# The sum of the second row blocks and the residual of down by accumulating transfers, and a new order of first casts and sums in a Strassen-Winograd feed-forward network

## What is computed

```python
h = x + jnp.concatenate([a, c], axis=-1) @ w_out
n2 = rms_norm(h, norm_ffn)
h = h + (jax.nn.silu(n2 @ w_gate) * (n2 @ w_up)) @ w_down
# D_MODEL 2048, D_FF 5632, 544 tokens
y = rms_norm(h, norm_final)
```

## Time and profile before

| | us |
|---|---|
| time, median of 3 runs | 2389.84 (2389.76 to 2390.09) |
| the profiled execution | 2386.59 |
| its span, first to last instruction | 2384.9 |
| TensorE busy | 2285.8 (96%) |
| VectorE busy | 1830.2 (77%) |
| ScalarE busy | 991.9 (42%) |
| POOL busy | 496.6 (21%) |
| share of the 16 DMA engines, SP's queue and POOL's | 40.7% and 3.8% |

### The profile page before, as it was taken

How to read it: one execution, slowest core, us unless ns; L and a number is a source line. 1 busy time by engine, 2 the same in 40 slices (tenths; PEclk the granted TensorE clock), 3 DMA queues, 4 the chain that set the end, 5 groups by cost and what they waited for, 6 DMA issues and landing times.

```text
span 2384.9 us, 48272 instructions
## 1 busy us (share of the span) xinstructions
PE 2285.8 (96%) x17572; PEld 2192.5 (92%) x17572; DVE 1830.2 (77%) x2648; ACT 991.9 (42%) x1409; POOL 496.6 (21%) x528
## 2 busy tenths in 40 slices
PE   7999999999989997999999999999999789999898
PEld 6977999998759997999999999999999789989898
DVE  5688999997624558877777777778777788888897
ACT  6154344333532224444444444444444343443444
POOL 2324899650550102010100101010010000000000
PEclk9999999999999998999999999999999899999999
DMA  7414223323695452443444434444344653444543
GB/s 260 119 35 124 73 79 85 88 71 95 199 310 166 126 148 80 125 125 104 132 124 125 130 106 122 124 131 127 111 116 126 205 186 99 139 146 135 150 107 102
DMA packets 455375, 307.42 MB, mean 129 GB/s; under 512 B 23195, under 2 KB 436371, under 8 KB 454576
## 3 DMA queue, kind: packets, MB, share of 16 engines
q1 hardware_dynamic: 443472, 276.73, 40.7%
q0 software_dynamic: 11792, 29.23, 3.8%
HBM read 269.56 MB, written 37.18 MB: 129 GB/s over the span
## 4 chain that ended last, share of the span: by engine, by line
PE 55%; DVE 3%; issue 2%; ACT 1%; DMA 0%; POOL 0%; DVEq 0%; POOLq 0%; SPq 0%; ACTq 0%
PE ps L2452 54%; ACT opH L1160 1%; DVE wr L1843 1%; DVE opH L1869 1%; DVE h L1989 0%; DVE opX L1795 0%; DVE wl L1852 0%; PE ps L2501 0%; DVE wp L1819 0%; DMA h<-xT_dram 0%; ACT opX L1127 0%; POOL td L830 0%; DVE ws L1843 0%; DVE wr L1812 0%; DVE t L1900 0%
## 5 line engine op out<-in xcount | busy, mean ns | idle before, releaser
L2452 PE MATMUL ps<-opX,wp 128*128 128x272 f32 x7392 | 937.0, 290 | 12.1 <-ACT t L1170 9.5
L2452 PEld LDWEIGHTS ps<-opX,wp 128*128 128x128 f32 x7392 | 936.0, 189 | 12.8 <-ACT t L1170 9.9
L2452 PE MATMUL ps<-opH,wh 128*128 128x272 f32 x2464 | 468.9, 290 | 36.8 <-DVE h L1989 33.3
L1819 DVE TENSOR_TENSOR wp<-wr,wp 128x1024 fp32r<-128x1024 f32 x264 | 320.1, 1226 | 188.2 <-ACT wp L1143 185.9
L2452 PEld LDWEIGHTS ps<-opH,wh 128*128 128x128 f32 x2464 | 389.8, 190 | 40.6 <-DVE h L1989 36.6
L2074 PE MATMUL ps<-xs,whi 128*128 128x272 f32 (+1 forms) x2368 | 396.2, 289 | 6.4 <-DVE xs L1318 2.3
L2452 PE MATMUL ps<-opH,wl 128*128 128x272 f32 x1232 | 356.7, 290 | 0.0
L1143 ACT CAST wp<-wr 128x1024 fp32r<-128x1024 f32 x264 | 273.6, 1053 | 181.6 <-DVE wr L1812 140.0
L2074 PEld LDWEIGHTS ps<-xs,whi 128*128 128x128 f32 (+1 forms) x2368 | 334.7, 187 | 9.3 <-DVE xs L1318 2.8
L1154 ACT CAST wh<-wr 128x768 fp32r<-128x768 f32 (+1 forms) x192 | 149.8, 781 | 251.8 <-PE ps L2452 178.2
L2074 PE MATMUL ps<-xs,wlo 128*128 128x272 f32 (+1 forms) x1184 | 244.7, 288 | 0.0
(11 more groups left out here) (335 smaller groups left out, 2674.8 us busy)
## 6 DMA issues: line engine op xcount, KB each, us to landing
wr<-in_w_gate SPq DMA_DIRECT2D x88, 512.0 KB, 4.6
wr<-in_w_up SPq DMA_DIRECT2D x88, 512.0 KB, 7.1
raw<-in_w_in SPq DMA_DIRECT2D x72, 512.0 KB, 3.9
wr<-in_w_down SPq DMA_DIRECT2D x96, 384.0 KB, 5.4
rawH<-hid_dram SPq DMA_DIRECT2D x21, 816.0 KB, 6.7
raw<-in_w_out SPq DMA_DIRECT2D x32, 512.0 KB, 5.3
hid_dram<-hid SPq DMA_DIRECT2D x88, 136.0 KB, 1.8
hid_dram<-td SPq DMA_DIRECT2D x66, 136.0 KB, 1.8
```

The costliest lines, as they stand in the source:

```text
L1819: ve.tensor_tensor(w[:, 1, :, :], src[:, :, :], w[:, 0, :, :].bitcast(F32), ALU.subtract).then_inc(s_wlo, 1)
L2452: ins = te.matmul(prod_bank(par, i), w[:, t, :], op[:, x, t, :], start=(i in (0, 1, 3) and t == 0 and w is whi_ and x == 0), stop=(t == kk ...
```

## The change

Three parts.

At the start of gate and up, ScalarE squares tile 14 first, casts pieces 4 and 5 before the weights of unit 2, and takes unit 0's result earlier. VectorE sums and splits in a matching order, and does B21 - B11 in one operation of 2176 columns; POOL's two operations for it go.

In the first group of down, h isn't loaded first. ScalarE copies the results of units 0, 1, 2 and 6 into h (`placed`), VectorE adds units 3, 4 and 5, and POOL then adds the residual of each two tiles from `xT_dram` by an accumulating transfer (`residual_added`), one per pair. SP's three transfers go. The first additions of the second group wait for them.

In all of down, POOL fills ws2: a transfer of block 2, a wait, an accumulating transfer of block 3 (`second_row_sum`). It waits until VectorE has used the ws2 of the pair before. VectorE's sum for it goes. SP loads the same four blocks as before.

```diff
+        def adds(p):
+            return 3 * min(p, NP2) + 7 * max(p - NP2, 0)
...
-            sp.wait_ge(s_prod, fed(NP1 - 1, 6))
-            sp.dma_start(h[:, 0:2, :], xT_dram[:, 0:2, :]).then_inc(s_xr[0], 16)
-            sp.dma_start(h[:, 2:8, :], xT_dram[:, 2:8, :]).then_inc(s_xr[1], 16)
...
-            sp.dma_start(h[:, 8:16, :], xT_dram[:, 8:16, :]).then_inc(s_hl, 16)
...
-            operand_sums(B21, B21, B11, ALU.subtract, 0, 7)
-            pool.wait_ge(s_opl, 8)
-            operand_sums(B21, B21, B11, ALU.subtract, 7, 8)
...
+            def second_row_sum(p):
+                ws = ws2[:, 0:KG[p // NP2], :]
+                if p == 0:
+                    pool.wait_ge(s_wlo, fed(NP1 - 2, 6))
+                else:
+                    pool.wait_ge(s_wlo, fed(NP1 + p - 1, 1))
+                    pool.wait_ge(s_wsum, sums2(p - 1) + 2)
+                pool.dma_start(ws, down_block(p, 2)).then_inc(s_ws, 16)
+                pool.wait_ge(s_ws, AT_SW + 32 * p + 16)
+                pool.dma_start(ws, down_block(p, 3), accum_op=ALU.add).then_inc(s_ws, 16)
+            def residual_added(i):
+                if i:
+                    pool.wait_ge(s_hres, AT_SW + 16 * i)
+                pool.wait_ge(s_hcp, 4 * i + 4)
+                pool.wait_ge(s_hacc, adds(i + 1))
+                pool.dma_start(h[:, 2 * i:2 * i + 2, :], xT_dram[:, 2 * i:2 * i + 2, :], accum_op=ALU.add
+                               ).then_inc(s_hres, 16)
+            second_row_sum(0)
             hid_sums(NB2 - 1)
+            second_row_sum(1)
+            for s in range(2):
+                pool.wait_ge(s_xw[s], AT_XW + 16 * 8)
+            for p in range(2, 4 * NP2):
+                second_row_sum(p)
+                if p < NP2 + 2:
+                    residual_added(p - 2)
...
+            square_of(14, 0)
             weight_high1(0, 0, 0, 1)
-            square_of(14, 0)
             weight_high1(0, 1, 0, 1)
-            weight_high1(0, 2, 0, 1)
...
             piece_high(6)
+            taken(t1[:, 0:HALF], 0, 0, 0)
+            weight_high1(0, 2, 0, 1)
             piece_high(7)
+            weight_high1(0, 3, 0, 1)
...
+            def placed(p, k):
+                e, n, t = p % 2, NP1 + p, 2 * p
+                unit_, tile_, half = ((0, t, slice(0, HALF)), (1, t + 1, slice(HALF, NT)), (2, t, slice(HALF, NT)),
+                                      (6, t + 1, slice(0, HALF)))[k]
...
+                act.wait_ge(s_prod, fed(n, unit_))
+                nc.scalar.copy(h[:, tile_, half], prod_bank(e, unit_)).then_inc(s_hcp, 1)
...
+                    if c == 0 and v in (0, 1, 2, 6):
+                        placed(p, min(v, 3))
...
-                dst, x, z, op = ((ws2, raw4[2], raw4[3], ALU.add), (raw4[2], raw4[0], raw4[2], ALU.subtract),
-                                 (raw4[0], ws2, raw4[0], ALU.subtract), (raw4[1], raw4[1], raw4[0], ALU.subtract))[k]
+                dst, x, z = ((raw4[2], raw4[0], raw4[2]), (raw4[0], ws2, raw4[0]), (raw4[1], raw4[1], raw4[0]))[k]
...
-            weight_sum1(0, 2, 0)
             piece_low(4)
             piece_low(5)
             dve.wait_ge(s_mm, 2 * M_FFN)
             residual(15, 1, 16 * 8)
-            for x in range(6, 8):
-                piece_low(x)
+            weight_sum1(0, 2, 0)
+            piece_low(6)
             weight_low1(0, 2, 0)
+            piece_low(7)
+            weight_low1(0, 3, 0)
+            piece_low(8)
+            weight_low1(0, 4, 0)
+            weight_sum1(0, 3, 0)
+            dve.wait_ge(s_xd, 8)
+            dve.wait_ge(s_opl, 9)
+            ve.tensor_tensor(B21, B21, B11, ALU.subtract).then_inc(s_xd, 1)
+            piece_low(9)
...
-                    else:
+                    elif c or v in (3, 4, 5):
                         gathered(p, v)
...
+                if c == 0:
+                    dve.wait_ge(s_hcp, 4 * p + after)
+                elif after:
+                    dve.wait_ge(s_hacc, adds(p) + after)
+                elif c == 1:
+                    dve.wait_ge(s_hres, AT_SW + 16 * (i + 1))
```

More of the change, by code:

```diff
@@ L69 @@
 NPIECE = 11
-AT_OPD = AT_HL = 32 * 6
+AT_OPD = AT_SW = 32 * 6
 AT_WR = 32 * 8
@@ L320, in build @@
         s_ho0, s_ho = s_iks[2:4]
-        s_hl = s_pg[9]
         s_opd = s_pg[2:9]
-        s_hacc = sem("s_hacc")
+        s_hacc, s_hcp = sem("s_hacc"), sem("s_hcp")
+        s_hres, s_ws = s_pgp[2:4]
         s_gf, s_yt, s_ya, s_yd = (sem("s_" + x) for x in ("gf", "yt", "ya", "yd"))
@@ L491, in op_slot, with sums2, down_block @@
             return (7 * c + j) % 9
+        def adds(p):
+            return 3 * min(p, NP2) + 7 * max(p - NP2, 0)
+        def sums2(p):
+            return 4 * NP1 + 3 * p
+        def down_block(p, b):
+            c, i = divmod(p, NP2)
+            return w_down[:, b % 2, KG0[c]:KG0[c] + KG[c], 256 * i + P * (b // 2):256 * i + P * (b // 2) + P]
         def fed(n, i):
@@ L1148, in weight_high2 @@
                 act.wait_ge(s_prod, fed(n, i) - (3 if v > 2 else 4))
-                if SUM[i]:
-                    act.wait_ge(s_wsum, 4 * n + SUM[i])
+                if i == 1:
+                    act.wait_ge(s_ws, AT_SW + 32 * p + 32)
+                elif SUM2[i]:
+                    act.wait_ge(s_wsum, sums2(p) + SUM2[i])
                 else:
@@ L1205, in pair1 @@
                 after = extra or (lambda k: None)
-                taken(t1[:, 0:HALF], par, 0, n)
-                weight_high1(par, 3, n, fill)
+                if extra is not first_extra:
+                    taken(t1[:, 0:HALF], par, 0, n)
+                    weight_high1(par, 3, n, fill)
                 after(0)
@@ L1253, in final_square @@
             def final_square(j):
-                act.wait_ge(s_hacc, 7 * (3 * NP2 + j // 2) + (6, 7)[j % 2])
+                act.wait_ge(s_hacc, adds(3 * NP2 + j // 2) + (6, 7)[j % 2])
                 act.wait_ge(s_sqs, KT + 2 + max(j - 1, 0))
                 nc.scalar.activation(sqf[:, j % 2, :], h[:, j, :], ACT.Square).then_inc(s_sqh, 1)
+            def placed(p, k):
+                e, n, t = p % 2, NP1 + p, 2 * p
+                unit_, tile_, half = ((0, t, slice(0, HALF)), (1, t + 1, slice(HALF, NT)), (2, t, slice(HALF, NT)),
+                                      (6, t + 1, slice(0, HALF)))[k]
+                if k == 0 and p == 5:
+                    act.wait_ge(s_ho0, AT_HO + 16 * NB2)
+                    act.wait_ge(s_ho, AT_HO + 96 * NB2)
+                act.wait_ge(s_prod, fed(n, unit_))
+                nc.scalar.copy(h[:, tile_, half], prod_bank(e, unit_)).then_inc(s_hcp, 1)
             for p in range(4 * NP2):
@@ L1904, in pair1 @@
                 after = extra or (lambda k: None)
-                weight_low1(par, 3, n)
-                weight_sum1(par, 3, n)
-                after(0)
-                weight_low1(par, 4, n)
-                after(1)
+                if extra is not first_extra:
+                    weight_low1(par, 3, n)
+                    weight_sum1(par, 3, n)
+                    after(0)
+                    weight_low1(par, 4, n)
+                    after(1)
                 weight_low1(par, 5, n)
@@ L2488, in _ @@
                 else:
-                    pe.wait_ge(s_hacc, 7 * (p - 1))
+                    pe.wait_ge(s_hacc, adds(p - 1))
+                    if p < NP2 + 2:
+                        pe.wait_ge(s_hcp, 4 * (p - 1))
                 for i in range(7):
-                    if i in (2, 4, 5, 6):
-                        pe.wait_ge(s_hacc, 7 * p + (1, 3, 3, 5)[(2, 4, 5, 6).index(i)])
+                    if c == 0:
+                        if i in (2, 4):
+                            pe.wait_ge(s_hcp, 4 * p + i - 1)
+                        if i == 6:
+                            pe.wait_ge(s_hacc, adds(p) + 2)
+                    elif i in (2, 4, 5, 6):
+                        pe.wait_ge(s_hacc, adds(p) + (1, 3, 3, 5)[(2, 4, 5, 6).index(i)])
                     if p % NP2 == 0:
```

58 lines of the change are left out of this document (20 added, 38 removed).

## The result

The changed kernel takes **2409.8 us** (median of 4 runs, 2403.2 to 2411.8) against 2389.8 before: ratio 1.0076, 95% interval 1.0063 to 1.0089. It is slower by 20 us where 12.6 us of gain were forecast. Its profiled execution, 2403.17 us with a span of 2401.3, is the fastest of the four, so it shows 16.6 us of the loss against the profiled execution of before (2386.59). The page of the changed kernel: share of the span by engine, transfers by queue, issues with KB each and us to landing.

What follows compares the result with a forecast made beforehand. TensorE was taken as full in mid-stage, so only some 48 us of its gaps could be had. 4.5 + 5.1 - 3 + 4.8 + 4.2 - 3 = 12.6 us gained, from 2389.84 to 2377 us; range 2364 to 2410.

Steps and rivals of the forecast that it cites:

- the first change of group: Down, first cluster of gaps: ScalarE's copies and one sum less on VectorE gain 4.8 us, 1 us charged for late landings.
- the other two: Down, second and third change of group: VectorE's sum goes, 2.1 us each, 4.2 gained, 1 us charged per change.
- the third term: Down, the new loop through ws: a loss of 3 us in the forecast's sum.
- Part 1: Start of gate and up: VectorE's one-piece difference and reordered casts bring low parts earlier; gain 4.5 us, bounds 2.5 and 6.9.
- Part 2: Entry of down: the 12.03 us gap shrinks, then ws of pair 1 is late; gain 5.1 us of 8.7, bounds 0 and 10.
- Part 3: Down: two-transfer ws loop just fits the first group's pairs; 0.5 us lost per pair over six, 3 us, bounds 0 and 13.
- Part 4: Down, three changes of group: less VectorE work gains 4.8 and 4.2 us, 1 us charged per change, 3 us.
- What was called free: Down: dropped SP residual transfers, POOL's new waits, the second group's residual wait and TensorE's changed waits were said to cost nothing.
- The slower one: Down: accumulates take 7 and 9.5 us, ws paces every pair, 27 us lost, about 2409 us; chance 0.26.

Runs made afterwards that it cites:

- e10: Kernel before with only the new start of gate and up (difference of B21 on VectorE, ScalarE's new order of casts): 2386.6 us, ratio 0.9993.
- e1: Changed kernel without the eight accumulating residual transfers in the first group of down: 2396.3 us, ratio 1.0029.
- e8: Changed kernel with the two ws transfers of pair 1 moved ahead of POOL's last sums of hid: 2407.7 us, ratio 1.0085.
- e2: Changed kernel with all sums into ws2 back on VectorE, the adding residual kept: 2379.2 us, ratio 0.9956.
- e7: Changed kernel with all ws sums back on VectorE and the adding residual moved from the first group to the second: 2375.5 us, ratio 0.9940.
- e5: Changed kernel with the second transfer of ws plain, overwriting instead of adding: 2395.1 us, ratio 1.0024.
- e4: Changed kernel with the residual's accumulating transfers moved from the first group to the second: 2403.8 us, ratio 1.0067.
- e3: Changed kernel with VectorE summing ws in the first group only, POOL's transfers in the later groups: 2385.4 us, ratio 0.9980.

## Why the prediction was wrong, point by point

The forecast's sum against what the profiled executions show, us gained: the start 4.5 and 5.0; the entry 5.1 and -0.5; the loop -3 and -17.4; the first change of group 4.8 - 1 and -3.9; the other two 4.2 - 2 and, with all later lengths, -0.5. With 1 us from the stage ahead that is -16.3. The failed step is the third term.

**Part 1, the start: right at its place.** 4.0 us measured with part 1 alone (e10), 5.0 in the changed kernel, 4.5 said; that they reach the end isn't shown. VectorE's 4.48 us piece beside POOL is gone; the changed kernel's timeline of VectorE at that place:

```profile
916.10 0.43 DVE L1842 TENSOR_TENSOR opX<-hg,opX 128x272 fp32r<-128x272 f32 x1
916.45 1.22 DVE L1866 TENSOR_TENSOR wp<-wr,wp 128x1024 fp32r<-128x1024 f32 x1
918.13 2.42 DVE L1842 TENSOR_TENSOR opX<-hg,opX 128x2176 fp32r<-128x2176 f32 x1 [0.46 <-ACT opX L1157]
```

**Part 2, the entry: the mechanism right, the gain not.** Without ws on POOL's queue the first two lengths fall from 36.5 to 28.2 us, 8.3 of the 8.7 said. With it they are 36.9: nothing gained, where 5.1 were said. I let ws of pair 1 land 3.4 + 4.8 us after POOL got free. I had placed the wait right (a gap of 4.51 us through a cast of ws), but the adding transfer was issued in the same microsecond as SP's loads of pair 2 and took 7.7 us. In e1, with no residual at all, it took 7.5 at this place, so it is stretched beside SP's loads without the residual. The changed kernel, transfers issued from 1868.0 to 1868.2 us:

```profile
wr<-in_w_down SPq DMA_DIRECT2D x2, 256.0 KB, 3.2
ws<-in_w_down POOLq DMA_DIRECT2D x1, 256.0 KB, 7.7
```

I had read SP's next loads at 1880.5, the time of before, and didn't move them forward with the entry that the change itself moves. e8 shows the place: there length 1 is 5.7 us shorter. A second length of 11.4 instead of 10.5 took another 0.9.

**Part 3, the loop through ws: this step failed.** The prices of the transfers were right, undisturbed 4.4 to 5.0 us for 256 KB (4.8 said) and 5.5 to 6.0 for 384 KB (6.2 said). So was the claim that the middle of the later groups hides the loop: 22 lengths sum to 364.9 against 364.4. (One price was right by luck: the 0.4 us for POOL's issue don't follow from their row. By the same working 128 KB from SP land after 2.3 us and POOL's after 2.4, which is 0.1 us more.) What failed is the first group: 3 us charged, with a bound of 13; lengths 3 to 6 alone lost 17.4 us. Two terms were wrong, the second far more.
- The loop: 10.9 us, not 10.4. From landing to the next issue it takes 2.7 us in e1 (1886.81 to 1889.50 us), not 2.2, and POOL needs 0.3 us between the two transfers, which I had left out. That alone puts it above a pair's 10.50. By itself it is what the 0.5 us per pair were charged for: lengths 3 to 5 of e1 lose 1.3 us together.
- The engines' time, which I never summed. I compared landings taken from undisturbed rows and read "39% busy" as room. SP's loads of one pair, in the kernel before, over 10.5 us (1889 to 1899.5):

```profile
q1 hardware_dynamic: 2112, 1.05, 34.2%
```

That is 3.6 us of the engines. The plain ws takes 1.0 and the adding one 2.2. The adding residual, in e2 over 6.4 us (1882.2 to 1888.6), its 272 packets, partly beside SP's:

```profile
q0 software_dynamic: 272, 0.56, 57.4%
```

3.7 us, and about the same in e7 (56.5% of 6.5 us from 2020.3) with hardly any other traffic. The sum is 10.5 us in a pair of 10.5. The changed kernel agrees: 75% of 42 us for 262 matmuls is 10.1 us of the engines for a pair's 84 matmuls.

With a pair's time on the engines all taken, transfers meet in every pair, and landings stretch. The changed kernel, transfers issued from 1907.6 to 1908.0 us:

```profile
wr<-in_w_down SPq DMA_DIRECT2D x2, 256.0 KB, 3.3
ws<-in_w_down POOLq DMA_DIRECT2D x1, 256.0 KB, 8.3
```

Both landings of ws in each of the four slow rounds, plus the 3.0 us of the loop that are no landing (2.7 + 0.3), give the lengths, in us:

| length | plain ws | adding ws | with 3.0 | measured | e1: the same sum | e1 measured |
|---|---|---|---|---|---|---|
| 3 | 4.7 | 4.6 | 12.3 | 12.1 | 11.3 | 11.2 |
| 4 | 5.5 | 8.3 | 16.8 | 16.7 | 10.9 | 10.7 |
| 5 | 5.0 | 4.4 | 12.4 | 12.6 | 11.0 | 10.9 |
| 6 | 8.4 | 6.6 | 18.0 | 18.0 | 15.9 | 15.9 |

So the loop paces these pairs, and late landings are the loss: 15.9 us of the 17.4 are landings beyond 3.4 and 4.5. Not every landing is late. In lengths 3 to 5 the plain ones are, each issued before the residual has landed (by 0.3, 3.2 and 0.4 us); the adding one of length 4 is, beside SP's loads. In length 6 both are, beside the operand loads; there they are late in e1 too (7.1 and 5.8 us). ScalarE's casts of ws show it:

```profile
1887.30 0.62 ACT L1186 CAST wh<-ws 128x512 fp32r<-128x512 f32 x1 [0.88 <-PE ps L2501]
...
1899.42 0.62 ACT L1186 CAST wh<-ws 128x512 fp32r<-128x512 f32 x1 [2.50 <-DMA ws<-in_w_down]
...
1916.08 0.62 ACT L1186 CAST wh<-ws 128x512 fp32r<-128x512 f32 x1 [7.74 <-DMA ws<-in_w_down]
...
1928.69 0.62 ACT L1186 CAST wh<-ws 128x512 fp32r<-128x512 f32 x1 [1.72 <-DMA ws<-in_w_down]
```

Seen from TensorE, 12.3 of the 17.4 us are three gaps (0.35, 5.29, 6.64) and the rest goes with the lower granted clock, 0.91 from 1888 to 1948. This is crowding and loop together, and neither alone: less adding (e5), less residual (e1, e4) and both transfers of ws away (e2) give back 11.3, 12.7 and 29.4 us of the nine lengths, more in sum than was lost, as it is when several things must come together for the loss. No run separates the DMA engines from the memory behind them.

**Part 4, the changes of group: half right.** In the first one ScalarE's copies work: with no ws or residual transfers beside it, lengths 7 to 9 fall from 50.1 to 47.3 us (e7), 2.8 gained; 4.8 were said with VectorE's sum gone too, worth 0.9 of it. In the changed kernel they are 54.0: the plain ws issued at 1961.59 us landed after 6.2 us and the adding one behind it after 12.3, beside the operand and weight loads. In the second change (lengths 14 to 17) the two lengths with the small gaps shrink as said, 17.0 to 16.7 and 20.5 to 19.6, but the length ahead of them grows from 15.7 to 16.3 and the one behind from 18.1 to 18.7. 2.1 us said, 1.2 came and 1.2 went. The third (22 to 25) is 0.6 us longer than before. So the two later changes brought about nothing where 2.2 us net were said. Over the seven kernels with POOL's sums in the later groups the 22 lengths sum to 363.2 to 370.5 us, mean 367.6, over the other seven, with VectorE's sums near the changes, to 364.4 to 367.4, mean 365.7. So POOL's sums cost about 1 us per change on average, though the two sets overlap; the charge had the right size and the gain didn't come.

**What was called free.** "POOL's new waits have nothing behind them but its own transfers" was the costly sentence: the next ws is one of those transfers, and the residual stands in front of it and takes 3.7 us of the engines.

**The rivals.** The slower one gave 2409 us, very near the time, for a wrong reason: that is luck. It wanted a slow adding transfer (7 and 9.5 us) that paces all 30 pairs. The transfer is fast, the later 22 lengths are unharmed, and the loss lies in nine. Its threshold, 4.9 us for 256 KB, was the useful part: it is what landings of 6.6 and 8.3 us under load go beyond. I gave it 0.26 and the sum went with undisturbed prices.

## What to carry to other kernels

When a change puts a transfer into a loop that holds its buffer, add up two things per round: the loop with landings taken beside the other traffic, and the engines' time of every queue (share times window), the added transfers included. Here the quiet price didn't hold where a transfer met SP's loads (7.5 us instead of 4.5, even without the residual), and with the second sum at a whole round something met in every round. The loop that "just fits" passed the late landings straight on. Transfers that nobody waits for soon, like the residual here, filled the engines to 78% at no cost in mid-group. So give the adding transfers to stages with slack and keep them away from the loads of the next stage.

## What the runs showed of the hardware

- An adding transfer holds the engines more than twice as long: 2.2 us instead of 1.0 for 256 KB, 528 packets instead of 80. The number of packets isn't the reason: SP's four plain loads of this size are 2112 packets, 528 each, and take 0.9 us each, so a packet takes 27 ns plain and 65 adding. For 384 KB, in the middle of a later group of e3 (windows of 4.4 and 5.9 us):

```profile
q0 software_dynamic: 112, 0.39, 34.1%
...
q0 software_dynamic: 784, 0.39, 54.3%
```

1.5 and 3.2 us. The Trainium skill ("Collectives: The Full Stack", The bandwidth ceiling) puts the adding transfers of a ReduceScatter, two reads and one write, at half the rate of a copy; the engines' time here agrees, 2.1 times a copy's. The landing rises by a third only, 3.4 to 4.5 us.
- POOL's row for issuing an adding transfer is longer, 1.29 us against 0.77, and 1.74 for the residual. But the next issue begins 0.77 us after it, within the row, so it isn't shown that POOL is held for longer. The changed kernel's timeline of POOL, plain ws, adding ws, adding residual:

```profile
1878.40 0.77 POOL L862 DMA_DIRECT2D ws<-in_w_down  x1 [9.00 <-DVE wr L1889]
1882.00 1.29 POOL L864 DMA_DIRECT2D ws<-in_w_down  x1 [2.82 <-DMA ws<-in_w_down]
1882.77 1.74 POOL L872 DMA_DIRECT2D h<-xT_dram  x1
```
